# Hybrid encoder layer on eight cores: spatial gate in other PSUM banks, weight casts moved to a block's start, DMA transposes issued apart from their norm weights

## The chip, the cores and the metric

The kernel runs as one program on the 8 cores of one Trainium2 chip; every core has its own 10240 tokens, and the cores exchange nothing. A time is device microseconds (us) from start to end of the slowest core. The engines of a core are TensorE (PE, matmuls), VectorE (DVE), ScalarE (ACT), GpSimd (POOL) and SyncE (SP), and each works its own queue strictly in the program's order. A DMA is issued from a queue: here from SP, or from POOL where it changes the type.

## The reference, cut to what matters

```
h    = rmsnorm(x, norm_pre_mix)
proj = h @ W_in                       # [f | u | v | gate_a | gate_b], 512+512+512+1024+1024
u, v = gelu(u), gelu(v);  gate_a, gate_b = sigmoid(...), sigmoid(...)
y_a  = fourier_mix(f) @ w_fourier_out       # Re of a 2-D DFT
v    = layernorm(v)
y_b  = (u * (W_s v + b_s)) @ w_sgu_out      # spatial gate: W_s is 128x128 per group, in chunks of 128 positions
x    = x + rmsnorm((gate_a * y_a + gate_b * y_b) @ w_o, norm_post_mix)
h2   = rmsnorm(x, norm_pre_ffn)
up   = conv3(h2 @ w_up)                     # depthwise over positions
x    = x + rmsnorm((gelu(up[:4096]) * up[4096:]) @ w_down, norm_post_ffn)
```

D_MODEL is 1024, the mixer widths are 512, D_FF is 4096. Matmul operands are bf16, sums float32.

## The kernel before, in words

The program is written out in Python by `Prog.op`: each operation is appended to the queue of its engine, and waits are derived from the names that it reads and writes. So the order in the code is the order on each engine, and an operation that waits holds up everything behind it on its engine.

It has three stages. The Fourier stage (80 tiles of 128 tokens) ends in DRAM. The **mixer stage** is the loop `for p, i in enumerate(blocks)`: 20 blocks of 512 tokens, p = 0 to 19. The **channel stage** is 20 blocks of 32 column groups (`up`, `conv`), each followed by the down projection.

A mixer block p works so. SP loads `Yb` (the Fourier result) and the next block's four token tiles `xt`. PE forms four `u` chunks (`proj_chunk`, L838 to L844) and then four times a `v` tile (`v_tile`) and an output tile of block p-1 (`out_tile`). An output tile goes through `close_tile`: ACT squares it (L474), POOL takes the inverse root (L479, L481), DVE scales it (L924), POOL adds the residual `xr` (L929) and SP stores it to `x1s`. There are two `xr` buffers: the residual of tile 3 is loaded only after tile 1 is stored. ACT also squares the next block's tile (`pre_square`, L474 too). Behind tile 3's add POOL forms the next block's scales `rsd` (`pre_scale`: L479 and L481 on 128x4).

Then comes the gate phase, `for dc in range(8)`: chunk A (`winga`) and chunk B (`wingb`), each 8 matmuls into a bank that ACT empties by L843; in dc 0 and 1 also two spatial gates (`sgu_group`: 4 small matmuls, emptied by DVE L874, then DVE L881 with `uT`); and from dc = 2 the merge of dc - 2 (`merge_chunk`: 8 matmuls, DVE L891 and L895, POOL L898). In the text A0, B0, A1, B1 and so on are the gate chunks by dc. The banks: the projections and the spatial gates go round banks 1, 2, 3 (`wbank`); output tiles and merges use the pairs (4, 5) and (6, 7).

The next block is prepared inside the gate phase: `pre_cast(t)` (ACT L527) scales tile t to bf16 in `xs`, of which there are two, and waits for `rsd`; `pre_flip(t)` issues a DMA transpose from SP (L553) into `hT` and appends at once the DVE multiply with the norm weights (L555), which waits for that transfer. Casts stand at dc 2 to 5, flips at dc 3 to 6.

Blocks p = 1 to 3 also carry the second Fourier stage (`big_steps`), whose small matmuls use `wbank` too. From p = 4 each block converts a part of the channel stage's weights to bf16 in DRAM, by DMAs issued on POOL: `cast_wup` (L495, two DMAs) and `cast_wd` (L448). They stand behind `pre_scale`, at dc = 2 and at dc = 5.

Of the kernel before, what the change touches and what calls it, by code (L numbers as in the profile page):

```python
# [8 lines left out]
BF16 = mybir.dt.bfloat16  # L9
# [3 lines left out]
D = 1024  # L13
# [309 lines left out]
def build_program(cfg=None):  # L323
# [68 lines left out]

    NH = 2 * NBLK
    xt = [at(4 * k, D, F32, [("xt", k)]) for k in range(4)]
    xs = [at(16 + 2 * k, D, BF16, [("xs", k)]) for k in range(2)]
    hTb = [at(20 + 8 * k, 8 * 512, BF16, [("hT", k, t) for t in range(4)]).rearrange("p (k t) -> p k t", t=512)
           for k in range(2)]
    tt = [at(36 + 4 * k, D, F32, [("tt", k)]) for k in range(2)]
# [122 lines left out]
        s = pre_slot[par]  # L521
        inv_root(rsd[s][:, 0:4], ssq[s][:, 0:4], EPS, 4, [("ssq", s, t) for t in range(4)], ("rsd", s))

    def pre_cast(par, t):
        s = pre_slot[par]
        k = t % 2
        P.op("act", lambda e: e.activation(out=xs[k], in_=xt[t], func=AF.Copy, scale=rsd[s][:, t:t + 1]),  # L527
             reads=[("xt", t), ("rsd", s)], writes=[("xs", k)])

# [15 lines left out]
    def pre_turn(par, t, gvec, tbk=0):  # L545
        turn(t % 2, 128, hTb[par][:, :, t * 128:(t + 1) * 128], ("hT", par, t), gvec, tbk)

    def pre_flip(par, t, gvec):
        dst = hTb[par][:, :, t * 128:(t + 1) * 128]
        src = xs[t % 2]  # L550

        def flip(eng, sem):
            eng.dma_start_transpose(out=dst, in_=src).then_inc(sem, 16)  # L553
        P.op("sp", flip, reads=[("xs", t % 2)], writes=[("hT", par, t)], ndma=1)
        P.op("dve", lambda e: e.tensor_tensor(  # L555
            out=dst, in0=dst, in1=gvec.unsqueeze(2).broadcast_to([128, 8, 128]), op=ALU.mult),
            reads=[("hT", par, t), "cst0"], writes=[("hT", par, t)])

    def hres(par):
        return [("hT", par, t) for t in range(4)]  # L560
# [305 lines left out]
             reads=[("vg", k), ("mv", k), ("mvr", k)], writes=[("vhat", t)])  # L866

    def sgu_group(h):
        wb = wbank()
        for t in range(4):  # L870
            mm_group(bank(wb)[:, t * 128:(t + 1) * 128], [(vhat[:, t, h * 128:(h + 1) * 128], wstb[:, h, :])],
                     reads=[("vhat", t), "cstb"], writes=[("ps", wb)])
        k = ring("tmp", 4)
        P.op("dve", lambda e: e.scalar_tensor_tensor(  # L874
            out=tmp[k].rearrange("p (t q) -> p t q", q=128),
            in0=bank(wb).rearrange("p (t q) -> p t q", q=128),
            scalar=cst[:, C_LNG + h:C_LNG + h + 1],
            in1=bmat[:, h * 128:(h + 1) * 128].unsqueeze(1).broadcast_to([128, 4, 128]),
            op0=ALU.mult, op1=ALU.add),
            reads=[("ps", wb), "cst", "bmat"], writes=[("tmp", k)])  # L880
        P.op("dve", lambda e: e.tensor_tensor(out=uT[:, h, :], in0=tmp[k], in1=uT[:, h, :], op=ALU.mult),  # L881
             reads=[("tmp", k), ("uT", h)], writes=[("uT", h)])
# [108 lines left out]
    for p, i in enumerate(blocks):  # L991
# [10 lines left out]
        if p == 0:  # L1002
            next(big)
        else:
            pre_load(1 - par, nxt[0], nxt[1], nxt[2])
        for c in range(4):
            proj_chunk(par, winu, "winu", c * 128, uT[:, c, :], ("uT", c), AF.Gelu_apprx_tanh, 1.0)
            if p > 0:
                next(big, None)
# [15 lines left out]
            add()  # L1025
        if p > 0:
            pre_scale(1 - par)
        if p >= 4:
            cast_wup(1)
            cast_wd(1)  # L1030
        if p == NBLK - 1:
            ensure_loaded(NW - 1)
        for dc in range(8):
            h = dc // 2
            proj_chunk(par, winga, ("winga", h), dc * 128, ta[dc % NG], ("ta", dc % NG), AF.Tanh, 0.5)
            if dc < 2:
                sgu_group(2 * dc)
            if p > 0 or dc > 3:
                next(big, None)
            proj_chunk(par, wingb, ("wingb", h), dc * 128, tb[dc % NG], ("tb", dc % NG), AF.Tanh, 0.5)  # L1040
            if dc < 2:
                sgu_group(2 * dc + 1)
            if p == 0:
                if 1 <= dc < 5:
                    pre_square(1 - par, dc - 1)
                if dc == 4:
                    pre_scale(1 - par)
            late = 3 if p == 0 else 0
            if 3 + late <= dc < 7 + late:
                pre_flip(1 - par, dc - 3 - late, nxt[3])  # L1050
            if 2 + late <= dc < 6 + late:
                pre_cast(1 - par, dc - 2 - late)
            if dc >= 2:
                merge_chunk(dc - 2)
            if p > 0 or dc > 3:
                next(big, None)
            if p >= 4 and dc == 2:
                cast_wd(1)
            if p >= 4 and dc == 5:
                cast_wup(1)  # L1060
            if p == NBLK - 1 and dc == 7:
                halo_load(0)
        merge_chunk(6)
        next(big, None)
        if p == 0:
            pre_flip(1 - par, 2, nxt[3])
            pre_cast(1 - par, 3)
        merge_chunk(7)
        next(big, None)
        if p == 0:  # L1070
            pre_flip(1 - par, 3, nxt[3])


    cw4 = cst[:, C_CW:C_CW + 192].rearrange("p (h j t) -> p h j t", h=2, t=3)
# [74 lines left out]
    for i in range(NBLK):  # L1149
        more = i + 1 < NBLK  # L1150
        par = 1 - i % 2
        for j in range(32):
# [24 lines left out]
            if more:  # L1177
                if j in (8, 10, 12, 14):
                    pre_square(par, (j - 8) // 2)
                if j == 14:  # L1180
                    pre_scale(par)
                if j in (20, 22, 24, 26):
                    pre_flip(par, (j - 20) // 2, gpf)
                if j in (18, 20, 22, 24):
                    pre_cast(par, (j - 18) // 2)
        pending()
        pending = None
        r = ring_ctr.get("uppair", 0) % 3
# [115 lines left out]
```

## Time and profile before

| | us |
|---|---|
| median of 3 runs | 5149.03 |
| lowest and highest run | 5138.63, 6016.25 |
| the profiled execution's own time | 5129.78 |
| its span on the slowest core (core 6) | 5128.2 |
| spans of the 8 cores | 5085.4 to 5128.2 |
| mean granted TensorE clock of the cores | 0.992 to 0.994 |

The profile is one execution, seen on its slowest core. Outside the span lie 1.6 us. Its own time is 19 us under the median of the runs. In the rows an arrow points from what is waited for or read: `psum<-arena` writes PSUM from SBUF (the whole SBUF is one tensor, `arena`), and `[0.61 <-DVE arena L874]` is 0.61 us of idle time before the group, ended by the DVE instruction of line 874.

### The profile page before, as it was taken

The numbers are of one execution on the slowest core, as the hardware profiler recorded it, in microseconds if no ns is written. First come the engines' busy times: TensorE is split into PE (matmuls) and PEld (weight loads), VectorE is DVE, ScalarE is ACT, GpSimd is POOL, SyncE is SP. The second block draws the span as 40 slices with busy tenths as digits, with TensorE's granted clock in tenths as the row PEclk, the third lists the DMA queues.
The fourth block names the chain that finished last, engine by engine and source line by source line (L and its number), as shares of the span: only waits on it lengthen the run. The fifth ranks groups of instructions, "written<-read, shape, count | busy, mean of one in ns | idle before, by whom it ended". The sixth has DMA issues, their size and how long they took to land.

```text
span 5128.2 us, 81411 instructions; the slowest of 8 cores (5085.4 to 5128.2 us)
## 1 busy us (share of the span) xinstructions
PE 4970.4 (97%) x23976; PEld 2307.1 (45%) x24457; DVE 2786.6 (54%) x3917; ACT 2310.8 (45%) x3516; POOL 1984.9 (39%) x2480
## 2 busy tenths in 40 slices
PE   7889999999999999999999999999999999999999
PEld 4434444444444444444444444444444444444444
DVE  4635444444454475556645674557655674557554
ACT  5634433433333354445544554445544554445433
POOL 2323344443444433333433343334433343334333
PEclk9999999999999999999999999999999999999999
DMA  9794566555655574434534454445444454435432
GB/s 289 251 181 130 160 128 126 138 135 124 136 128 141 127 238 143 141 124 161 165 136 137 130 189 134 142 127 165 154 138 128 147 177 136 144 124 177 145 124 98
DMA packets 476173, 771.36 MB, mean 150 GB/s; under 512 B 285751, under 2 KB 310455, under 8 KB 474590
## 3 DMA queue, kind: packets, MB, share of 16 engines
q1 hardware_dynamic: 384526, 689.65, 43.3%
q0 software_dynamic: 91216, 76.46, 8.1%
q8 instruction: 210, 3.44, 0.3%
q14 instruction: 221, 1.81, 0.1%
HBM read 655.27 MB, written 130.02 MB: 153 GB/s over the span
## 4 chain that ended last, share of the span: by engine, by line
PE 89%; DMA 5%; issue 3%; POOL 1%; DVE 1%; ACT 1%; SPq 0%; POOLq 0%; DVEq 0%; ACTq 0%
PE psum L463 67%; PE psum L1194 21%; DMA arena<-arena 1%; DMA arena<-xf 1%; DMA arena<-xn 1%; ACT arena L474 0%; POOL arena L929 0%; PE psum L725 0%; DMA arena<-zbig 0%; DVE arena L874 0%; POOL arena L481 0%; DMA x1s<-arena 0%; DMA zbig<-arena 0%; POOL arena L714 0%; SPq L448 0%
## 5 line engine op out<-in xcount | busy, mean ns | idle before, releaser
L463 PE MATMUL psum<-arena 128*128 128x512 bf16 (+3 forms) x18278 | 3838.0, 369 | 108.2 <-DVE arena L874 15.3
L463 PEld LDWEIGHTS psum<-arena 128*128 128x128 bf16 (+1 forms) x18657 | 1767.3, 99 | 2152.4 <-issue 136.2
L1123 DVE SCALAR_TENSOR_TENSOR arena<-psum,arena 128x511 f32<-128x511 f32 x2560 | 1751.0, 743 | 348.7 <-ACT arena L1111 348.5
L1111 ACT ACTIVATE arena<-psum,arena 128x512 f32<-128x512 f32 x1280 | 993.2, 776 | 746.6 <-PE psum L463 746.6
L1133 POOL TENSOR_TENSOR arena<-arena 128x512 bf16<-128x512 bf16 x640 | 745.7, 1165 | 939.7 <-ACT arena L1131 922.1
L1194 PE MATMUL psum<-arena 128*128 128x512 bf16 x5018 | 1102.8, 379 | 5.4
L924 DVE SCALAR_TENSOR_TENSOR arena<-psum,arena 128x1024 f32<-128x1024 f32 x159 | 204.1, 1284 | 1154.6 <-POOL arena L481 1145.9
L1194 PEld LDWEIGHTS psum<-arena 128*128 128x128 bf16 x5120 | 500.9, 98 | 603.9
L474 ACT ACTIVATE arena<-psum 128x1024 bf16<-128x1024 f32 x160 | 163.8, 1024 | 1157.6 <-PE psum L1194 958.7
L843 ACT ACTIVATE arena<-psum 128x512 bf16<-128x512 f32 x400 | 238.5, 596 | 640.9 <-PE psum L463 609.7
L929 POOL TENSOR_TENSOR arena<-arena 128x1024 f32<-128x1024 f32 x159 | 377.0, 2371 | 189.9 <-DVE arena L924 126.6
L1131 ACT ACTIVATE arena<-arena 128x512 bf16<-128x512 f32 x640 | 397.0, 620 | 65.3 <-POOL arena L1128 64.2
L479 POOL TENSOR_SCALAR arena<-arena 128x1 f32<-128x1 f32 (+2 forms) x241 | 52.2, 216 | 946.8 <-ACT arena L474 940.5
L898 POOL TENSOR_TENSOR arena<-arena 128x512 bf16<-128x512 f32 x160 | 226.0, 1413 | 452.2 <-DVE arena L895 452.1
L555 DVE TENSOR_TENSOR arena<-arena 128x1024 bf16<-128x1024 bf16 x156 | 199.1, 1276 | 238.6 <-DMA arena<-arena 238.6
L1128 POOL TENSOR_TENSOR arena<-arena 128x4 f32<-128x4 f32 x640 | 197.0, 308 | 270.8 <-DVE arena L1123 265.2
L474 ACT ACTIVATE arena<-arena 128x1024 bf16<-128x1024 f32 (+1 forms) x241 | 253.3, 1051 | 38.1 <-DMA arena<-xf 26.9
L527 ACT ACTIVATE arena<-arena 128x1024 bf16<-128x1024 f32 x160 | 182.3, 1139 | 32.3 <-DMA arena<-arena 31.7
L891 DVE SCALAR_TENSOR_TENSOR arena<-arena,psum 128x512 f32<-128x512 bf16 x160 | 109.5, 684 | 127.8 <-PE psum L463 123.6
L481 POOL TENSOR_TENSOR arena<-arena 128x1 f32<-128x1 f32 (+2 forms) x241 | 159.3, 661 | 35.7
L854 DVE BATCH_NORM_STATS2 arena<-arena 128x6 f32<-128x512 f32 x80 | 54.9, 686 | 158.3 <-ACT arena L852 158.3
L895 DVE SCALAR_TENSOR_TENSOR arena<-arena,psum 128x512 f32<-128x512 bf16 x160 | 109.5, 684 | 12.7 <-PE psum L463 3.7
(45 smaller groups left out, 975.7 us busy)
## 6 DMA issues: line engine op xcount, KB each, us to landing
arena<-wups SPq DMA_DIRECT2D x640, 512.0 KB, 3.5
arena<-xn SPq DMA_DIRECT2D x160, 512.0 KB, 6.6
arena<-x1s SPq DMA_DIRECT2D x160, 512.0 KB, 5.5
arena<-xf SPq DMA_DIRECT2D x40, 1024.0 KB, 11.7
x1s<-arena SPq DMA_DIRECT2D x80, 512.0 KB, 3.2
y<-arena POOLq DMA_DIRECT2D x79, 512.0 KB, 4.0
wups<-w_up POOLq DMA_DIRECT2D x64, 256.0 KB, 5.2
arena<-yscr SPq DMA_DIRECT2D x20, 512.0 KB, 4.0
```

The costliest lines, as they stand in the source:

```text
L463: ins = e.matmul(out, lhsT=l, rhs=r, start=(i == 0), stop=(i == n - 1))
L474: P.op("act", lambda e: e.activation(out=sqjunk[:n, :], in_=src, func=AF.Square, accum_out=acc), reads=reads, writes=["sqjunk", accname])
L555: P.op("dve", lambda e: e.tensor_tensor(out=dst, in0=dst, in1=gvec.unsqueeze(2).broadcast_to([128, 8, 128]), op=ALU.mult), reads=[("hT", p ...
L843: P.op("act", lambda e: e.activation(out=dst, in_=bank(wb), func=func, scale=scale), reads=[("ps", wb)], writes=[dres])
L898: P.op("pool", lambda e: e.tensor_tensor(out=mT[:, dc, :], in0=tmp[k1], in1=tmp[k2], op=ALU.add), reads=[("tmp", k1), ("tmp", k2)], writes ...
L924: P.op("dve", lambda e: e.scalar_tensor_tensor(out=tt[k], in0=po, scalar=rsd2[s2][:, 0:1], in1=gpo, op0=ALU.mult, op1=ALU.mult), reads=pr ...
L929: P.op("pool", lambda e: e.tensor_tensor(out=xr[k2], in0=tt[k], in1=xr[k2], op=ALU.add), reads=[("tt", k), ("xr", k2)], writes=[("xr", k2)])
L1111: P.op("act", lambda e, half=half, b=b, c=c: e.activation(out=cv2[:, half, :], in_=bank(b), func=AF.Identity, bias=cst[:, C_CB + c:C_CB + ...
L1123: P.op("dve", lambda e, o_=o_, i_=i_, wt=wt: e.scalar_tensor_tensor(out=o_, in0=i_, scalar=wt, in1=o_, op0=ALU.mult, op1=ALU.add), reads=[ ...
L1131: P.op("act", lambda e: e.activation(out=gg, in_=cv2[:, 0, :], func=AF.Gelu_apprx_tanh), reads=[("cgv", k, 0)], writes=[("gg", k)])
L1133: P.op("pool", lambda e: e.tensor_tensor(out=actT[:, j, :], in0=gg, in1=cv2[:, 1, :], op=ALU.mult), reads=[("gg", k), ("cgv", k, 1)], writ ...
L1194: P.op("pe", lambda e, dh=dh: [e.matmul(bank(b0 + dh), lhsT=actT[:, j, t * 128:(t + 1) * 128], rhs=wd[j // 4][:, j % 4, dh * 512:(dh + 1) ...
```

## The change

It touches the mixer stage, and the channel stage's preparation of the next block.

- Spatial gate h goes to bank 4 + h (those of output tiles and merges) and no longer to the ring of banks 1 to 3.
- The four weight casts of a block (p from 4) are issued in one piece behind `pre_load`, ahead of the `u` chunks.
- `pre_flip` issues only the DMA transpose; the multiply is a function of its own, `pre_gain`.
- There are four `xs` tiles (two of them lie where the second Fourier stage had its buffer, so they are used from p = 4 on).
- For p = 4 to 18 cast and flip of tile t stand at dc = t (0 to 3) and the multiply at dc = t + 4. For p = 1 to 3 and 19: cast and flip at dc = t + 1, multiply at dc = t + 3, with two `xs`.
- In block p = 0 the transposes are made on PE again (`pre_turn`, 8 transposes of 128x128 and a DVE multiply out of bank 0).
- In the channel stage casts and flips stand one j earlier (17, 19, 21, 23), the multiplies where they were.

```
 def pre_cast(par, t, nx=2):            # xs[t % nx]
+def pre_gain(par, t, gvec):
     dst = hTb[par][:, :, t * 128:(t + 1) * 128]
-    src = xs[t % 2]
-    ...
-    P.op("sp", flip, reads=[("xs", t % 2)], writes=[("hT", par, t)], ndma=1)
     P.op("dve", lambda e: e.tensor_tensor(
         out=dst, in0=dst, in1=gvec.unsqueeze(2).broadcast_to([128, 8, 128]), op=ALU.mult), ...)
+def pre_flip(par, t, nx=2):
+    ...
+    P.op("sp", flip, reads=[("xs", t % nx)], writes=[("hT", par, t)], ndma=1)

 def sgu_group(h):
-    wb = wbank()
+    wb = 4 + h

@@ mixer block
+        if p >= 4:
+            cast_wd(1)
+            cast_wup(1)
+            cast_wd(1)
+            cast_wup(1)
         for c in range(4):
             proj_chunk(par, winu, ...)
@@
-        if p >= 4:
-            cast_wup(1)
-            cast_wd(1)
@@ for dc in range(8)
-            late = 3 if p == 0 else 0
-            if 3 + late <= dc < 7 + late:
-                pre_flip(1 - par, dc - 3 - late, nxt[3])
-            if 2 + late <= dc < 6 + late:
-                pre_cast(1 - par, dc - 2 - late)
+            if p == 0:
+                if 6 <= dc:
+                    pre_turn(1 - par, dc - 6, nxt[3])
+                if 5 <= dc:
+                    pre_cast(1 - par, dc - 5)
+            elif 4 <= p < NBLK - 1:
+                if dc < 4:
+                    pre_cast(1 - par, dc, 4)
+                    pre_flip(1 - par, dc, 4)
+                else:
+                    pre_gain(1 - par, dc - 4, nxt[3])
+            else:
+                ...
             if dc >= 2:
                 merge_chunk(dc - 2)
-            if p >= 4 and dc == 2:
-                cast_wd(1)
-            if p >= 4 and dc == 5:
-                cast_wup(1)
```

The order on ACT, for one block with p from 4 on, from the last output tile to the fourth cast. L474 are the squares, L843 the gate chunks in the order A0, B0, A1, B1 and so on, L527 the casts. Before:

```order
L474 ACTIVATE arena<-psum 128x1024
L474 ACTIVATE arena<-arena 128x1024
L843 ACTIVATE arena<-psum 128x512 x6
L527 ACTIVATE arena<-arena 128x1024
L843 ACTIVATE arena<-psum 128x512 x2
```

Now (L846 is what was L843):

```order
L474 ACTIVATE arena<-psum 128x1024
L474 ACTIVATE arena<-arena 128x1024
L846 ACTIVATE arena<-psum 128x512 x2
L527 ACTIVATE arena<-arena 128x1024
L846 ACTIVATE arena<-psum 128x512 x2
```

The first cast stood behind six gate chunks and now stands behind two.

The order on POOL, for the end of one block's preparation (L479 and L481 on 128x4 form `rsd`) and its eight merges (L898). Before:

```order
L929 TENSOR_TENSOR arena<-arena 128x1024 x2
L479 TENSOR_SCALAR arena<-arena 128x4
L481 TENSOR_TENSOR arena<-arena 128x4
L495 DMA wups<-w_up 1024x1x128 x2
L448 DMA wds<-w_down 16x8192
L898 TENSOR_TENSOR arena<-arena 128x512
L448 DMA wds<-w_down 16x8192
L898 TENSOR_TENSOR arena<-arena 128x512 x3
L495 DMA wups<-w_up 1024x1x128 x2
L898 TENSOR_TENSOR arena<-arena 128x512 x4
L857 TENSOR_SCALAR arena<-arena 128x1
```

Now (L932 was L929, L901 was L898, L860 was L857):

```order
L932 TENSOR_TENSOR arena<-arena 128x1024 x2
L479 TENSOR_SCALAR arena<-arena 128x4
L481 TENSOR_TENSOR arena<-arena 128x4
L901 TENSOR_TENSOR arena<-arena 128x512 x8
L448 DMA wds<-w_down 16x8192
L495 DMA wups<-w_up 1024x1x128 x2
L448 DMA wds<-w_down 16x8192
L495 DMA wups<-w_up 1024x1x128 x2
L860 TENSOR_SCALAR arena<-arena 128x1
```

All six cast DMAs of a block now stand between the last merge and the next block's first `v` tile (L860); `rsd` stands where it stood.

## Rows read from the trace of the kernel before

**Rows 1.** Busy time per stage; columns: window, length, busy of each engine, clock, DMA share, GB/s
```profile
560.00:1780.00 1220.00, 1184.55 (x5572) 545.29 (x5684) 568.93 (x746) 458.02 (x737) 543.16 (x594) 0.99 0.58 132
1780.00:5128.00 3348.00, 3311.70 (x15551) 1515.31 (x15862) 1936.44 (x2747) 1571.84 (x2309) 1269.52 (x1644) 1.00 0.45 147
```

**Rows 2.** What PE waited for, window 560 to 1780; us in total, times, longest
```profile
PE psum L463 <- DVE arena L874: 15.3, 22, 1.5
PE psum L463 <- DVE arena L891: 10.2, 6, 3.7
```

**Rows 3.** PE's work in order of time; start, us, matmuls, in brackets the idle before
```profile
333.61 9.42 PE L463 MATMUL psum<-arena 128*128 128x512 bf16 x43 [2.38 <-DVE arena L470]
349.19 1.44 PE L463 MATMUL psum<-arena 128*128 128x512 bf16 x3 [6.16 <-DVE arena L555]
...
661.11 48.91 PE L463 MATMUL psum<-arena 128*128 128x512 bf16 x219 [2.11 <-DVE arena L891]
...
1168.00 49.99 PE L463 MATMUL psum<-arena 128*128 128x512 bf16 x219 [3.65 <-DVE arena L891]
1218.60 4.06 PE L463 MATMUL psum<-arena 128*128 128x512 bf16 x24 [0.61 <-DVE arena L874]
...
1387.29 47.23 PE L463 MATMUL psum<-arena 128*128 128x512 bf16 x219 [1.79 <-DVE arena L891]
```

**Rows 4.** The window around one long wait of PE, same columns as rows 1
```profile
1162.00:1174.00 12.00, 8.30 (x25) 3.09 (x25) 7.62 (x10) 3.38 (x4) 4.96 (x3) 0.72 0.64 77
```

**Rows 5.** The chain that ended last, from two late flips; start, us, what
```profile
720.62 12.66 DMA arena<-arena
...
1150.71 15.22 DMA arena<-arena
```

**Rows 6.** All DMA transposes of the program: count, median us from issue to landing
```profile
arena<-arena SPq DMA_TRANSPOSE x156, 4.2
```

**Rows 7.** The gate phase's start in the block at 1214, all but PE in order of time
```profile
1213.63 0.33 SPq L448 DMA_DIRECT2D x1s<-arena  x1
1214.25 1.02 ACT L474 ACTIVATE arena<-psum 128x1024 bf16<-128x1024 f32 x1 [2.34 <-PE psum L463]
1216.36 0.33 SPq L448 DMA_DIRECT2D arena<-xn  x1
1216.51 1.28 DVE L924 SCALAR_TENSOR_TENSOR arena<-psum,arena 128x1024 f32<-128x1024 f32 x1 [1.31 <-POOL arena L481]
1217.87 0.60 ACT L843 ACTIVATE arena<-psum 128x512 bf16<-128x512 f32 x1 [0.78 <-PE psum L463]
1220.04 2.35 POOL L929 TENSOR_TENSOR arena<-arena 128x1024 f32<-128x1024 f32 x1 [1.31 <-DVE arena L874]
1223.13 1.02 POOL L481 TENSOR_TENSOR arena<-arena 128x4 f32<-128x4 f32 x1
1227.94 1.14 ACT L527 ACTIVATE arena<-arena 128x1024 bf16<-128x1024 f32 x1
```

**Rows 8.** The square of the last output tile and the end of rsd, two blocks
```profile
922.16 1.02 ACT L474 ACTIVATE arena<-psum 128x1024 bf16<-128x1024 f32 x1 [2.34 <-PE psum L463]
931.62 1.02 POOL L481 TENSOR_TENSOR arena<-arena 128x4 f32<-128x4 f32 x1
...
1136.08 1.02 ACT L474 ACTIVATE arena<-psum 128x1024 bf16<-128x1024 f32 x1 [2.34 <-PE psum L463]
1148.32 1.02 POOL L481 TENSOR_TENSOR arena<-arena 128x4 f32<-128x4 f32 x1
```

**Rows 9.** DMA in windows of one block: its start, the lull, the stores, the casts
```profile
1186.00:1198.00 12.00, 11.95 (x57) 5.43 (x56) 2.10 (x4) 2.99 (x5) 3.04 (x4) 1.00 0.81 307
1198.00:1208.00 10.00, 9.95 (x47) 4.57 (x47) 4.99 (x7) 5.50 (x10) 4.18 (x7) 1.00 0.00 0
1208.00:1216.00 8.00, 8.00 (x42) 3.75 (x40) 3.39 (x7) 4.41 (x8) 5.25 (x10) 1.00 0.53 197
1226.00:1237.00 11.00, 10.95 (x52) 4.96 (x51) 1.38 (x2) 4.78 (x7) 2.13 (x3) 1.00 1.13 134
```

More of the change, by code:

```diff
@@ L394, in build_program @@
     xt = [at(4 * k, D, F32, [("xt", k)]) for k in range(4)]
-    xs = [at(16 + 2 * k, D, BF16, [("xs", k)]) for k in range(2)]
+    xs = [at((16, 18, 60, 62)[k], D, BF16, [("xs", k)]) for k in range(4)]
     hTb = [at(20 + 8 * k, 8 * 512, BF16, [("hT", k, t) for t in range(4)]).rearrange("p (k t) -> p k t", t=512)
@@ L522, in pre_scale, with pre_cast @@
         inv_root(rsd[s][:, 0:4], ssq[s][:, 0:4], EPS, 4, [("ssq", s, t) for t in range(4)], ("rsd", s))
-    def pre_cast(par, t):
+    def pre_cast(par, t, nx=2):
         s = pre_slot[par]
-        k = t % 2
+        k = t % nx
         P.op("act", lambda e: e.activation(out=xs[k], in_=xt[t], func=AF.Copy, scale=rsd[s][:, t:t + 1]),
@@ L546, in pre_turn @@
         turn(t % 2, 128, hTb[par][:, :, t * 128:(t + 1) * 128], ("hT", par, t), gvec, tbk)
-    def pre_flip(par, t, gvec):
+    def pre_gain(par, t, gvec):
         dst = hTb[par][:, :, t * 128:(t + 1) * 128]
-        src = xs[t % 2]
-        def flip(eng, sem):
-            eng.dma_start_transpose(out=dst, in_=src).then_inc(sem, 16)
-        P.op("sp", flip, reads=[("xs", t % 2)], writes=[("hT", par, t)], ndma=1)
         P.op("dve", lambda e: e.tensor_tensor(
@@ L557, in pre_flip, with flip @@
             reads=[("hT", par, t), "cst0"], writes=[("hT", par, t)])
+    def pre_flip(par, t, nx=2):
+        dst = hTb[par][:, :, t * 128:(t + 1) * 128]
+        src = xs[t % nx]
+        def flip(eng, sem):
+            eng.dma_start_transpose(out=dst, in_=src).then_inc(sem, 16)
+        P.op("sp", flip, reads=[("xs", t % nx)], writes=[("hT", par, t)], ndma=1)
     def hres(par):
@@ L1047, in build_program @@
                     pre_scale(1 - par)
-            late = 3 if p == 0 else 0
-            if 3 + late <= dc < 7 + late:
-                pre_flip(1 - par, dc - 3 - late, nxt[3])
-            if 2 + late <= dc < 6 + late:
-                pre_cast(1 - par, dc - 2 - late)
+            if p == 0:
[10 more added lines that the diff above has]
+            else:
+                if 1 <= dc < 5:
+                    if dc >= 3:
+                        pre_gain(1 - par, dc - 3, nxt[3])
+                    pre_cast(1 - par, dc - 1)
+                    pre_flip(1 - par, dc - 1)
+                elif 5 <= dc < 7:
+                    pre_gain(1 - par, dc - 3, nxt[3])
             if dc >= 2:
@@ L1065, in build_program @@
         if p == 0:
-            pre_flip(1 - par, 2, nxt[3])
+            pre_turn(1 - par, 2, nxt[3])
             pre_cast(1 - par, 3)
@@ L1070, in build_program @@
         if p == 0:
-            pre_flip(1 - par, 3, nxt[3])
+            pre_turn(1 - par, 3, nxt[3])
     cw4 = cst[:, C_CW:C_CW + 192].rearrange("p (h j t) -> p h j t", h=2, t=3)
@@ L1182, in build_program @@
                 if j in (20, 22, 24, 26):
-                    pre_flip(par, (j - 20) // 2, gpf)
-                if j in (18, 20, 22, 24):
-                    pre_cast(par, (j - 18) // 2)
+                    pre_gain(par, (j - 20) // 2, gpf)
+                if j in (17, 19, 21, 23):
+                    pre_cast(par, (j - 17) // 2)
+                    pre_flip(par, (j - 17) // 2)
         pending()
```

## The prediction

> **What bounds the kernel now.** I read the stages by windows first, then the list of what PE waits for, then PE's work in order of time, and last ACT, POOL and the DMAs around the gate phase. The channel stage takes 3348 us of the span, and PE is busy for 3311.7 of them at a granted clock of 1.00 [rows 1]: what hides behind PE there can be moved freely, and nothing is to be won. The mixer window has 1220 us with 1184.6 busy, so 35.5 us in which PE waits [rows 1]. That is all that this change can take away there. Two entries make up most of it: 15.3 us in 22 waits on the spatial gate's emptying (DVE L874), and 10.2 us in 6 waits on the merge's emptying (DVE L891) [rows 2].
>
> The first comes from the ring of three banks. In the row at 1218.60 PE has idled 0.61 us for L874: the gate group holds the bank that the next gate chunk wants, and its emptying stands on DVE behind L924 of the last output tile [rows 3]. The list has 22 of them: one in each of the 16 blocks from p = 4 on, and a second one behind it in six.
>
> The second is a transfer. In two blocks the first flip took 12.66 and 15.22 us [rows 5], where the median of all is 4.2 [rows 6]. DVE stands at L555 for it with the merge's L891 behind, and PE runs out of banks: 2.11 and 3.65 us of waiting at 661.11 and 1168.00 [rows 3]. While the weight casts run, just before and under the flips, the DMA share is 1.13 [rows 9].
>
> **A wait has a price beyond its length.** Around the 3.65 us wait the granted clock is 0.72 over a window of 12 us [rows 4], so for part of it the chip granted 1.2 GHz where the rest ran at 2.4. The 219 matmuls behind it took 49.99 us and the 219 behind a 1.79 us wait took 47.23 [rows 3]: 2.8 us more. Behind the 2.11 us wait it is 48.91, which is 1.7 more. Behind 1.79 us, nothing was added.
>
> **The change part by part.**
>
> *Spatial gate in banks 4 to 7.* The ring waits go: 15.3 us [rows 2]. The new banks are those of output tiles 2 and 3, and L924 of tile 3 is over at 1217.79, 3.5 us after the gate phase's start [rows 7], ahead of gate 2's matmuls at 5.8 (three chunks and two groups, below), so no new wait. Saving 15.3.
>
> *Transposes apart from the multiplies, casts of weights elsewhere.* With the multiply four dc later (some 20 us) DVE no longer stands before a transfer. The 10.2 us [rows 2] go, and with them the clock's 1.7 and 2.8 us. Saving 14.7. The DVE work is the same and only later.
>
> *Block p = 0 on PE.* PE waited 2.38 and then 6.16 us for flips there [rows 3]. Four turns of 8 transposes are bounded by 0.2 us (nearly half of what eight matmuls of 128 columns take, so a floor) and 1.73 us (a whole chunk) apiece; I take 0.6, nearer the small matmuls, so 2.4 us. The last turn still needs the last cast and has a multiply behind it, so I leave a third of the 6.16 us standing at the start of block 1, 1.9 us. 8.5 less 4.3 is 4.2, and with 2.8 us of clock saved (one wait like the 3.65 one) it is 7.
>
> *The six cast DMAs of a block, now ahead of u.* POOL spends a few us on issuing them; it has nothing to do there, between the last merge and the first `v` tile. The transfers meet the loads of `Yb`, `xt` and `xr`, which fill 0.81 of the engines for 12 us, and then run into ten empty microseconds [rows 9]. In the window of the casts 1.13 of the engines were busy for 11 us, and this was more than half of a block's casts; I put a block's casts at 15 us of all engines. Loads (0.81 times 12, 9.7 us) and casts together are busy for 25 us, and the gate phase begins some 27 us after the block's start (1187 to 1214). So the casts' end comes close to the stores and loads of the residuals, which begin some 6 us before the gate phase (the window from 1208 [rows 9]). I take 0.5 us per block, 7 in all, as they overlap little; the bounds are 0 and what a late flip lost, 15.22 less 4.2, that is 11 us [rows 5, 6].
>
> On this the Trainium skill has a rule that weighs the other way than the row: "DMA: Bandwidth & Descriptors", section "Queues, rings and completion order", says that each DMA engine takes turns between the queues it has work for, packet by packet. By it a store could lose only about its own length to casts. The flips lost 8 to 11 us with the casts in flight, which is more than turns explain [rows 5, 6]. By the rule the sum has 7 us here or less, by the row it is the slower rival below.
>
> *The token casts at dc = 0.* This is the new wait. The first cast waits for `rsd`. In the block whose gate phase begins at 1214.25 (the square of the last output tile), `rsd` is ready at 1224.15, 9.9 us later, while ACT emptied chunk B0 at 1217.87 [rows 7]. Before, the cast came at 1227.94, behind six chunks, and so stood behind `rsd` anyway. Now it stands behind B0, and behind it on ACT stand A1 and B1. PE needs A1's bank for B2, since the ring has three banks and the gates no longer turn it. PE reaches B2 after five chunks of 1.73 us (8 of the 219 matmuls that take 47.23 [rows 3]) and four gate groups of 0.22 us (4 matmuls with a quarter of the columns): 9.5 us after the start. The bank is free at `rsd` plus the cast (1.14) plus the emptying (0.60): `rsd` plus 1.75. So PE waits (`rsd` - 7.75) us, in each of the 15 blocks p = 4 to 18.
>
> `rsd` cannot come sooner: it ends a chain of tile 1's add, its store at 1213.63, the load of tile 3's residual at 1216.36, the add at 1220.04 and the root [rows 7]. None of this is changed. By its distance the 15 blocks fall in three classes: six at 9.8 to 10.5 (the blocks at 1214 [rows 7] and 922 [rows 8]), three at 11.0 to 11.5, and six at 12.8 to 13.8 (1136 [rows 8]). The waits are 2.6, 3.5 and 5.5 us: 6 x 2.6 + 3 x 3.5 + 6 x 5.5 = 59 us. Nothing hides them, since PE is the engine that sets the end. To this comes the clock: 1.7 us for the six short ones and 2.8 for the nine others gives 35, of which I take 28, as a wait of 1.79 us cost nothing.
>
> *Blocks 1 to 3 and 19, and the channel stage.* Casts at dc = 1 instead of 2 stand behind four chunks, where the same rule gives B3 as the chunk that waits, at about 15.6 us, later than `rsd` plus 1.75 even in the slowest class. Zero, with a bound of 2 us each way in blocks 1 to 3. In the channel stage PE covers it all: zero.
>
> **The sum.** Saved: 15.3 + 14.7 + 7 = 37. Added: 59 + 28 + 7 = 94. Net 57 us slower. Against the profiled execution's 5129.8 this is 5187; that execution lies 19 us under the median of the runs, so on their scale 5206, and as the 7 of contention and the clock's part are my softest terms I say 5200, one per cent slower. This is under the 2% (103 us) that a measurement of this kernel can about tell from no change.
>
> **The rivals.**
>
> *A, the cast doesn't hold PE (5112).* The gains come alone: 5149 - 37. For it: ACT is busy for 458 us of the 1220 [rows 1] and has room to catch up. Against it: `rsd` is ready 9.9 us after the start at the soonest, ACT is at the cast after 4.2 [rows 7], and A1 stands behind it. Only an `rsd` 2 us sooner than in any block would do it. 12%.
>
> *B, the wait is there but always short (5155).* If the long class of `rsd` (12.8 and more) is itself made by transfers that the move of the casts smooths, all 15 blocks wait about 2.5 us: 38, with 5 us of clock: 43 - 37 is +6. For it: the short class is as common as the long one. Against it: the windows with store and load had no casts of this core beside them before either (they come at 1226 [rows 9]). 18%.
>
> *C, the casts reach the residual's chain (5280).* Place: store of tile 0 and load of tile 2, store of tile 1 and load of tile 3. If the casts still run 6 us before the gate phase and delay it as they delayed the flips, `rsd` comes 4 us later on average and every wait grows by that: 15 x 4 = 60, and the clock takes its 2.8 us in each block instead of 28 in all, 14 more: +57 + 74 = +131. It decides from where loads and casts together are busy for more than 21 us after the block's start; I reckoned 25 with them overlapping well. For it: rows 5. Against it: the casts are issued 20 us ahead of the chain. 15%.
>
> **How the numbers follow.** 55% for the forecast (its own range 5165 to 5240), 12% for A, 18% for B, 15% for C. The range 5122 to 5272 leaves out most of A and the upper half of C. Slower by over 2% is C and a little of the forecast's tail, 0.14; faster by over 2% would need more than PE waits in the whole stage, 0.01; within 2% has 0.85.
>
> **What would show it.** In the profile after: no wait of PE on the spatial gate's emptying (now L877) from p = 4 on; almost none on the merge's (now L894); a new first entry, PE waiting for ACT's gate emptying (L846), some 15 times with 2 to 6 us each, 59 us in all; ACT's first cast (L527) idle for 5 to 9 us on POOL L481; clocks under 1.00 in the mixer windows; the channel stage unchanged at 3312 us of busy PE. If PE waits on ACT for under 20 us in the mixer stage, the forecast's main step is wrong. If `rsd` comes 15 us or more after the gate phase's start, C is right.

## The result, and the profile after

The changed kernel is slower: 1.0177 times the kernel before, 95% interval 1.0101 to 1.0254. The interval leaves open whether it is more than 2%. Two of its runs took 5227.55 and 5242.54 us; the other two, of 5602 and 5859 us, fell into executions in which a die runs slower whatever the kernel, and such executions of this and every other kernel are left out of all ratios and times below. The profiled execution has a span of 5226.0 us on its slowest core, again core 6, against 5128.2: 97.8 us more. The forecast was 5200, or 1.0% slower; so direction and place came out, and the size did not: 98 us where the sum had 57.

The windows of the changed kernel, with the columns of [rows 1]; the mixer stage now ends near 1880:

```profile
560.00:1880.00 1320.00, 1213.04 (x5671) 549.14 (x5669) 579.72 (x742) 453.37 (x738) 575.89 (x594) 0.96 0.54 121
1880.00:5226.00 3346.00, 3325.70 (x15850) 1514.05 (x15848) 1939.60 (x2746) 1568.79 (x2306) 1264.94 (x1641) 1.00 0.45 147
```

All of the loss lies in the mixer stage. PE idles for 107 us of its window, where it was 35.5, and the granted clock has gone from 0.99 to 0.96. The channel stage is as long as it was, 3346 us to 3348, so what was moved there shows no cost and no gain.

What PE waited for in the mixer stage of the changed kernel, against [rows 2]:

```profile
PE psum L463 <- ACT arena L846: 104.2, 16, 7.5
PE psum L463 <- POOL arena L901: 2.5, 1, 2.5
```

Both old entries are gone, and one new one has come, almost seven times as large as the larger of them. PE's work in order of time shows it once a block, against [rows 3]:

```profile
642.11 72.01 PE L463 MATMUL psum<-arena 128*128 128x512 bf16 x336 [6.82 <-ACT arena L846]
...
1195.48 71.81 PE L463 MATMUL psum<-arena 128*128 128x512 bf16 x336 [7.14 <-ACT arena L846]
1274.13 71.73 PE L463 MATMUL psum<-arena 128*128 128x512 bf16 x336 [6.85 <-ACT arena L846]
```

The 336 matmuls of a block now run without any other break; in the fifteen blocks p = 4 to 18 the break before them is 5.6 to 7.5 us.

The gate phase of the block that begins at 1257.91 (the square of the last output tile), all engines but PE, against [rows 7]:

```profile
1252.12 0.33 SPq L448 DMA_DIRECT2D x1s<-arena  x1
1258.52 0.33 SPq L448 DMA_DIRECT2D arena<-xn  x1
1258.94 0.38 SPq L448 DMA_DIRECT2D x1s<-arena  x1
1261.53 0.60 ACT L846 ACTIVATE arena<-psum 128x512 bf16<-128x512 f32 x1 [0.78 <-PE psum L463]
1262.81 2.35 POOL L932 TENSOR_TENSOR arena<-arena 128x1024 f32<-128x1024 f32 x1 [2.74 <-DMA arena<-xn]
1264.07 0.33 SPq L448 DMA_DIRECT2D arena<-xn  x1
1267.94 2.88 POOL L932 TENSOR_TENSOR arena<-arena 128x1024 f32<-128x1024 f32 x1 [2.78 <-DVE arena L877]
1271.24 1.02 POOL L481 TENSOR_TENSOR arena<-arena 128x4 f32<-128x4 f32 x1
1272.36 1.15 ACT L527 ACTIVATE arena<-arena 128x1024 bf16<-128x1024 f32 x1 [10.23 <-POOL arena L481]
1273.41 1.06 ACT L846 ACTIVATE arena<-psum 128x512 bf16<-128x512 f32 x2
```

Read it from below. PE went on at 1274.13, when ACT had emptied chunk A1, the first of the two at 1273.41. ACT came to that only after the token cast, for which it had stood 10.23 us. The cast waited for `rsd`, ready at 1272.26, 14.35 us after the phase's start, where [rows 7] have 9.9 and the longest before was 13.8. And `rsd` was late because of the two stores. Tile 0's was issued at 1252.12, and the load that waits for its landing (tile 2's residual) went out only at 1258.52: 6.4 us. On SP tile 1's store stands behind that load, so it too went out late, and the pair of this store and tile 3's load has 1258.94 and 1264.07, 5.1 us; in [rows 7] it is 1213.63 and 1216.36, 2.7 us.

The block of [rows 7] is one of the quickest of the kernel before. The means of the blocks p = 4 to 18, both on core 6, times from the gate phase's start, read from all stores and loads of the residual chain:

| | before | changed |
|---|---|---|
| tile 0's store: issue, time to landing | -5.8, 3.4 | -5.7, 6.1 |
| tile 2's load: issue, time to landing | -2.2, 4.1 | 0.6, 4.3 |
| tile 1's store: issue, time to landing | -0.6, 3.9 | 1.0, 5.1 |
| tile 3's load: issue, time to landing | 3.4, 3.8 | 6.2, 3.7 |
| `rsd` ready | 11.6 | 14.2 |

Both stores are slower, and on this core the loads hardly are. The issuing of the casts is not the cause: POOL had done with it by 1236.97 and then stood idle for DVE:

```profile
1240.71 0.19 POOL L860 TENSOR_SCALAR arena<-arena 128x1 f32<-128x1 f32 x1 [3.74 <-DVE arena L858]
```

The DMA windows of this block, against [rows 9]: the two windows ahead of the gate phase, and then the clock around PE's wait.

```profile
1241.00:1251.00 10.00, 10.00 (x48) 4.58 (x47) 4.33 (x6) 5.49 (x10) 4.06 (x8) 1.00 1.24 250
1251.00:1259.00 8.00, 8.00 (x39) 3.63 (x38) 4.05 (x8) 3.83 (x7) 5.58 (x8) 1.00 0.89 138
...
1265.00:1280.00 15.00, 8.15 (x34) 3.31 (x33) 4.62 (x7) 5.28 (x7) 4.25 (x4) 0.77 0.47 140
```

The ten empty microseconds are filled (0.00 to 1.24) and the stores' window is at 0.89 instead of 0.53, with less moved: 138 GB/s for 197. The page has the weight casts (`wups`) landing in a median 19.7 us and all stores to `x1s` in 3.8:

```profile
x1s<-arena SPq DMA_DIRECT2D x80, 512.0 KB, 3.8
...
wups<-w_up POOLq DMA_DIRECT2D x64, 256.0 KB, 19.7
```

The same rows of the kernel before:

```profile
x1s<-arena SPq DMA_DIRECT2D x80, 512.0 KB, 3.2
...
wups<-w_up POOLq DMA_DIRECT2D x64, 256.0 KB, 5.2
```

### The profile page after: what moved, and what is told of

Same layout as the page of the kernel before. It is cut to its first block, busy times and chain, and to the rows that moved or that the text cites. A ratio compares the mean times of both kernels' runs of the same rounds, so it can differ in the third digit from the quotient of the medians.

```text
span 5226.0 us, 81993 instructions; the slowest of 8 cores (5195.2 to 5226.0 us)
## 1 busy us (share of the span) xinstructions
PE 5039.4 (96%) x24489; PEld 2322.5 (44%) x24489; DVE 2803.4 (54%) x3917; ACT 2304.7 (44%) x3516; POOL 2022.5 (39%) x2480
## 4 chain that ended last, share of the span: by engine, by line
PE 87%; DMA 7%; POOL 3%; issue 2%; ACT 1%; SPq 0%; DVE 0%; POOLq 0%; ACTq 0%; DVEq 0%
PE psum L463 65%; PE psum L1210 21%; DMA x1s<-arena 3%; DMA arena<-xn 2%; POOL arena L932 2%; DMA arena<-xf 1%; POOL arena L481 1%; DMA arena<-zbig 1%; PE psum L728 1%; SPq L448 0%; ACT arena L474 0%; DMA yscr<-arena 0%; POOL arena L479 0%; ACT arena L846 0%; POOL arena L717 0%
## 5 line engine op out<-in xcount | busy, mean ns | idle before, releaser
L463 PE MATMUL psum<-arena 128*128 128x512 bf16 (+3 forms) x18657 | 3904.1, 372 | 149.8 <-ACT arena L846 104.8
L474 ACT ACTIVATE arena<-psum 128x1024 bf16<-128x1024 f32 x160 | 163.8, 1024 | 1157.5 <-PE psum L1210 959.1
L846 ACT ACTIVATE arena<-psum 128x512 bf16<-128x512 f32 x400 | 236.3, 595 | 611.3 <-PE psum L463 611.2
L901 POOL TENSOR_TENSOR arena<-arena 128x512 bf16<-128x512 f32 x160 | 263.8, 1649 | 529.7 <-DVE arena L898 529.6
L932 POOL TENSOR_TENSOR arena<-arena 128x1024 f32<-128x1024 f32 x159 | 375.9, 2364 | 235.5 <-DVE arena L927 126.6
L479 POOL TENSOR_SCALAR arena<-arena 128x1 f32<-128x1 f32 (+2 forms) x241 | 49.8, 207 | 953.3 <-ACT arena L474 946.9
L474 ACT ACTIVATE arena<-arena 128x1024 bf16<-128x1024 f32 (+1 forms) x241 | 253.3, 1051 | 32.9 <-DMA arena<-xf 21.6
L527 ACT ACTIVATE arena<-arena 128x1024 bf16<-128x1024 f32 x160 | 182.2, 1139 | 163.6 <-POOL arena L481 159.6
L481 POOL TENSOR_TENSOR arena<-arena 128x1 f32<-128x1 f32 (+2 forms) x241 | 159.2, 661 | 36.0 <-POOL arena L479 1.4
L857 DVE BATCH_NORM_STATS2 arena<-arena 128x6 f32<-128x512 f32 x80 | 54.8, 685 | 156.0 <-ACT arena L855 156.0
L898 DVE SCALAR_TENSOR_TENSOR arena<-arena,psum 128x512 f32<-128x512 bf16 x160 | 110.0, 687 | 22.9 <-PE psum L463 9.6
## 6 DMA issues: line engine op xcount, KB each, us to landing
arena<-xf SPq DMA_DIRECT2D x40, 1024.0 KB, 11.3
wups<-w_up POOLq DMA_DIRECT2D x64, 256.0 KB, 19.7
```

What stands on the lines that cost most here:

```text
L463: ins = e.matmul(out, lhsT=l, rhs=r, start=(i == 0), stop=(i == n - 1))
L474: P.op("act", lambda e: e.activation(out=sqjunk[:n, :], in_=src, func=AF.Square, accum_out=acc), reads=reads, writes=["sqjunk", accname])
L481: P.op("pool", lambda e: e.tensor_tensor(out=out, in0=out, in1=neghalf[:p, 0:n], op=ALU.pow), reads=[name, "neghalf"], writes=[name])
L846: P.op("act", lambda e: e.activation(out=dst, in_=bank(wb), func=func, scale=scale), reads=[("ps", wb)], writes=[dres])
L901: P.op("pool", lambda e: e.tensor_tensor(out=mT[:, dc, :], in0=tmp[k1], in1=tmp[k2], op=ALU.add), reads=[("tmp", k1), ("tmp", k2)], writes ...
L932: P.op("pool", lambda e: e.tensor_tensor(out=xr[k2], in0=tt[k], in1=xr[k2], op=ALU.add), reads=[("tt", k), ("xr", k2)], writes=[("xr", k2)])
```

## The experiments

Theory 1 is the prediction's: the token cast at dc = 0 waits on ACT for `rsd` and holds chunk A1's bank, and the weight casts lengthen the wait by delaying `rsd`. Rival 2: the weight casts' traffic is the cost by itself. Further rivals stand with the runs. For e1, e6, e8 and e12 there is no ratio; they stand beside 5121 to 5166 us for the kernel before, and the verdict rests on the trace. No difference below, up or down, is clear of 2%; where an interval leaves out 1, its sign is shown. Where means of the eight cores are given, they are of one profiled execution of each kernel; the fifteen blocks are p = 4 to 18, from block 4's gate phase to block 19's.

### e1: token casts back at dc 2 to 5

```
-                if dc < 4:
-                    pre_cast(1 - par, dc, 4)
-                    pre_flip(1 - par, dc, 4)
-                else:
-                    pre_gain(1 - par, dc - 4, nxt[3])
+                if dc >= 4:
+                    pre_gain(1 - par, dc - 4, nxt[3])
+                if 2 <= dc < 6:
+                    pre_cast(1 - par, dc - 2, 4)
+                    pre_flip(1 - par, dc - 2, 4)
```

> The changed kernel, but for p = 4 to 18 the token casts and flips stand at dc 2 to 5 again (multiplies stay at dc 4 to 7). Theory 1 (the token cast waits for rsd on ACT and holds chunk A1's bank): the 104 us of PE waiting on ACT's gate emptying go, with some 30 us of half clock; what was won elsewhere stays, so a span of 5085 to 5110 and a time about 1% under the kernel before. The end of rsd stays at 13 to 15 us after the gate phase's start. Rival 2 (the weight casts ahead of u are the cost by themselves, through the loads that they meet): the time stays near the changed kernel's 5227.

Measured: 5095.09 us, span 5093.5. PE's work from 600 us on, slowest core:

```profile
599.70 534.05 PE L463 MATMUL psum<-arena 128*128 128x512 bf16 x2566
1134.63 210.16 PE L463 MATMUL psum<-arena 128*128 128x512 bf16 x1008 [0.88 <-ACT arena L846]
1344.98 280.02 PE L463 MATMUL psum<-arena 128*128 128x512 bf16 x1344 [0.19 <-ACT arena L846]
```

The first stretch is 2566 matmuls without a break. Moving four casts by two dc takes away 132 us, and the weight casts stand where the change put them: rival 2 is out. `rsd` was later here than I expected and than in the changed kernel (15.4 to 18.7 us after the start on this core, the 18.7 in the block before 1134.63), and only behind the three latest does the cast at dc 2 cost anything, 0.88 us at most.

### e2: weight casts back in their old places

```
-        if p >= 4:                       # ahead of u
-            cast_wd(1); cast_wup(1); cast_wd(1); cast_wup(1)
+        if p >= 4:                       # behind pre_scale
+            cast_wup(1); cast_wd(1)
...
+            if p >= 4 and dc == 2: cast_wd(1)
+            if p >= 4 and dc == 5: cast_wup(1)
```

> The changed kernel with the weight casts back where they stood before (behind pre_scale, at dc 2 and dc 5). Theory 1: rsd ends 9.8 to 13.8 us after the gate phase's start again (mean 11.7 instead of 14.2), PE still waits for ACT's gate emptying once in each of 15 blocks, 2 to 6 us each, 60 us in all; a span near 5175. Rival 2: PE's waits on ACT go, span 5090 to 5110.

Measured: 1.0083 (1.0051 to 1.0116), span 5177.4.

```profile
PE psum L463 <- ACT arena L846: 68.8, 16, 6.0
```

This is the prediction's main sum by itself: 69 us of waits in a kernel whose `rsd` is not delayed (a mean of 12.0 us on this core). The changed kernel has 35 us of waits more, which is what the weight casts' new place costs as long as the token casts stand early. Of the 49 us of span between the two slowest cores 32 lie in the fifteen blocks; in the mean of the eight cores it is 39 of 44.

### e3: gate banks alone

```
 def sgu_group(h):
-    wb = wbank()
+    wb = 4 + h
```

> The kernel before with the spatial gate in banks 4 to 7 and nothing else. Theory 1: PE's 15 us of waiting on the spatial gate's emptying go and no new wait comes, 15 us faster (0.3%). Rival 3 (the gate in the output tiles' banks makes a new wait on L924 or holds the first merges): PE waits for DVE L924 or for the gate's emptying at the first merges, no gain.

Measured: 1.0001 (0.9983 to 1.0020). Neither theory had it:

```profile
PE psum L463 <- DVE arena L891: 20.3, 9, 4.9
```

The waits on the gate's emptying are gone and there is none on L924, but those on the merge's emptying have doubled against [rows 2]. This is not the choice of core: in the mean of the eight cores the gate's go from 12.0 us to 0 and the merge's from 6.7 to 14.7, and the fifteen blocks take 1068.4 us for 1071.0. Most of the wait was passed on, not removed. The chain that ended last shows what stands before the longest of them, which ends at 945.46, a flip that lands late:

```profile
932.04 12.33 DMA arena<-arena
944.63 0.69 DVE arena L891
```

PE comes to the merges sooner, and DVE stands at the same late transfer.

### e4: weight casts alone

The kernel before with the move of the diff of e2, the other way round.

> The kernel before with the weight casts ahead of u and nothing else. Theory 1: rsd ends 2.5 us later on average (near 14.2 us after the gate phase's start), but the first token cast stands at dc 2 and PE does not wait for it; the flips no longer meet the weight casts, so the 10 us on the merge's emptying go: 5110 to 5125, the same or slightly faster. Rival 2: 60 to 100 us slower.

Measured: 0.9964 (0.9940 to 0.9988).

```profile
PE psum L463 <- DVE arena L874: 15.8, 25, 1.3
PE psum L463 <- ACT arena L843: 3.4, 1, 3.4
...
PE psum L463 <- DVE arena L891: 1.5, 1, 1.5
```

As theory 1 has it, but for the size of the delay: I expected `rsd` at 14.2 us, and it has a mean of 15.3 on this core (14.3 over the eight, where the kernel before has 11.3). The same move of the same DMAs is a small gain where the token cast stands at dc 2. Its waits on the merge's emptying fall to 1.5 us since the flips no longer meet the weight casts. In one block tile 0's store went out at 1324.91 and the load behind it only at 1335.96, 11.05 us later:

```profile
1324.91 0.33 SPq L448 DMA_DIRECT2D x1s<-arena  x1
1335.96 0.33 SPq L448 DMA_DIRECT2D arena<-xn  x1
```

`rsd` was 22 us after the start there, and PE waited 3.4 us for ACT, the only time.

### e5 and e6: rsd sooner

```
-        if add is not None:
-            add()
         if p > 0:
             pre_scale(1 - par)
+        if add is not None:
+            add()
```

e5 is the changed kernel with this edit alone; e6 also has the weight casts in their old places.

> The changed kernel with pre_scale ahead of the last output tile's add on POOL (the two statements change places), nothing else. Theory 1: rsd no longer waits for the residual of tile 3; it ends behind the add of tile 2, some 9.2 us after the gate phase's start (14.2 before), so PE waits under 2 us in each of 15 blocks, 15 to 30 us in all, with little half clock: a time of 5105 to 5135. Rival 4 (ACT's order alone costs the time, whatever rsd does): PE's 104 us of waits stay, 5227.

> As the run before, with the weight casts also back where they stood before. Theory 1: rsd ends some 6 us after the gate phase's start, before PE would run out of banks at 7.5, so PE does not wait for ACT at all in blocks 4 to 18: 5080 to 5100. Rival 4: 5175.

Measured: e5 0.9941 (0.9918 to 0.9965), e6 5092.24 and 5098.44 us. e5's waits, then e6's work of PE (in the execution of 5098.44):

```profile
PE psum L463 <- ACT arena L846: 8.4, 7, 2.9
```

```profile
599.76 1092.76 PE L463 MATMUL psum<-arena 128*128 128x512 bf16 x5252
1706.21 19.57 PE L463 MATMUL psum<-arena 128*128 128x512 bf16 x80 [13.69 <-ACT arena L846]
```

The token casts stand at dc 0 in both, and almost nothing is lost: it was not ACT's order alone but the order together with a late `rsd`. e5 did better than forecast (`rsd` at 9.2 us and 15 to 30 us of waits): `rsd` has a mean of 7.6 us, and the longest wait that is left is in the block where it is latest (10.5 us, 2.95 us of waiting). Two statements that change places turn 1.8% slower into 0.6% faster. In e6 `rsd` ends 6.3 us after the start in every one of the 15 blocks, and PE makes 5252 matmuls in one stretch. Its one wait is in block 19, where there are only two `xs` tiles: its four flips took 26 us on SP beside the weight casts, and the third token cast stood for them with PE behind it. The wait is there on all eight cores (10.5 to 14.4 us); e5, whose weight casts stand ahead of u, has at most 1.8 us.

### e7: block 0's turns alone

`pre_turn` for `pre_flip` in p = 0.

> The kernel before with block 0's transposes on PE and nothing else. Theory 1: the waits of 2.4 and about 6 us of block 0 shrink to about 2 us in all, 4 to 7 us faster (0.1%). Rival 5 (the turns' PE and DVE time eats it): no difference.

Measured: 1.0005 (0.9989 to 1.0022), which can't tell 5 us from none. In the trace:

```profile
329.36 3.61 PE L463 MATMUL psum<-arena 128*128 128x128 bf16 x12 [2.63 <-DMA arena<-zbig]
...
348.49 13.80 PE L463 MATMUL psum<-arena 128*128 128x512 bf16 x79 [2.07 <-DVE arena L541]
```

One wait of 2.07 us stands at the start of block 1 for the 6.16 of [rows 3], as forecast, and the one of 2.38 is gone, but one of 2.63 for a transfer of the second Fourier stage stands near it, and the turns themselves take PE 2.7 us (0.61 to 0.84 each). In the mean of the eight cores block 4 begins at 620.0 us for 621.4. That is 1.4 us, less than two kernels differ that are alike up to there (e4 has 624.4), so whether the turns gain anything stays open.

### e8 and e11: separate multiplies, with and without the gate banks

e8 joins the edits of e1 and e2; e11 has `wb = wbank()` again besides.

> The changed kernel with the token casts and flips at dc 2 to 5 and the weight casts where they stood before; gate banks, separate multiplies and block 0's turns stay. Theory 1: rsd ends near 12 us after the gate phase's start and the cast stands at 12, so PE waits neither for ACT nor for the gate nor for the merge in blocks 4 to 18, blocks of 70.0 us: 5085 to 5105. If this is so, the move of the weight casts brings nothing that the separate multiplies don't bring. Rival 6 (the flips need to be free of the weight casts): late flips still hold PE through the multiplies, 15 us or more of waits on DVE, 5115 or more.

> As e8, but the gates go round banks 1 to 3 again. Theory 1: the waits on the gate's emptying are back, 0.6 us in each block and about 15 us in all, and those on the merge's emptying stay away: 5100 to 5120. Rival 8 (what the gate banks save is given back elsewhere, as in the run with the banks alone): the same time as e8.

Measured: e8 5091.31 us, span 5089.8; e11 0.9924 (0.9885 to 0.9963), span 5110.0. First a wait of DVE in e8, then the longest of PE in e11:

```profile
DVE arena L550 <- DMA arena<-arena: 139.3, 17, 11.6
```

```profile
PE psum L463 <- DVE arena L877: 11.1, 18, 0.9
```

In e8 the flips are as late as before (up to 14.9 us to landing), and DVE still stands at the multiply for up to 11.6 us, but no wait of PE follows from it:

```profile
599.76 1099.66 PE L463 MATMUL psum<-arena 128*128 128x512 bf16 x5284
```

The 15 blocks last 69.7 to 70.2 us from gate phase to gate phase. So rival 6 is out, and e1 and e8 being alike (5095 and 5091), the move of the weight casts brings nothing beside the separate multiplies. In e11 the 0.6 us per block on the gate are back, and its blocks last 70.7 us and more. Between e11 and e8 (5101 and 5091 us in the shortest times, 1062.7 and 1049.5 us for the fifteen blocks in the mean of the eight cores) the gate banks are worth what e3 could not show, since there another wait took it up: rival 8 is not borne out.

### e12: early token casts with the gates in the ring

e2 with `wb = wbank()`.

> As e11 (gates in the ring, weight casts in their old places, separate multiplies, block 0's turns), but the token casts and flips stand at dc 0 to 3. Theory 1: now the fourth gate group wants chunk A1's bank, two chunks sooner than B2 did: PE reaches it some 8.2 us after the gate phase's start, and the bank is free 1.75 us after rsd, so PE waits about rsd minus 6.4, with rsd near 12 some 5 to 6 us in each of 15 blocks, 80 to 90 us in all (69 in e2), and more half clock: a time of 5190 to 5225. Rival 9 (the wait is set by the number of chunks ahead of the cast alone and not by the banks): as e2, 5177.

Measured: 5268.99 us on core 4, with a granted clock of 0.972. Cores 0 to 3 have spans of 5183 to 5210 us at 0.984 to 0.986, and core 3 is read; the forecast of 5190 to 5225 can be held only against these:

```profile
620.56 3.84 PE L463 MATMUL psum<-arena 128*128 128x512 bf16 x20 [0.60 <-DVE arena L877]
629.83 68.73 PE L463 MATMUL psum<-arena 128*128 128x128 bf16 x316 [5.44 <-ACT arena L846]
```

```profile
PE psum L463 <- ACT arena L846: 84.2, 16, 9.0
```

The 20 matmuls before the long wait are A1, a gate group and B1, and the first form behind it is 128x128: PE waits at the fourth gate group, 8.2 us after the start. With `rsd` at 11.8 us in that block the rule gives 5.4 us, and 5.44 were measured; the waits sum to 84.2. The bank that is wanted next sets when an ACT queue hurts. Rival 9 is out. In this one respect the gate banks protected the changed kernel.

### e10 and e9: what is left

e10 is e5 with the token casts at dc 2 to 5; e9 is e8 with `pre_scale` first.

> The changed kernel with pre_scale ahead of the last add on POOL and the token casts at dc 2 to 5: the version that leaves neither wait. Theory 1: no wait of PE on ACT in blocks 4 to 18, 5080 to 5095, the fastest of all by some us. Rival 7 (the weight casts at the block's start still cost through another queue): no faster than 5100.

> As e8 (token casts at dc 2 to 5, weight casts in their old places), with pre_scale ahead of the last add. Theory 1: rsd ends 6.3 us after the gate phase's start, far ahead of the cast at 11.7; blocks of 70.0 us as in e8, so no more than a few us from e8 and e10: 5085 to 5100. It tells whether anything is left to win from rsd once the cast stands late: by theory 1 nothing.

Measured: e10 0.9912 (0.9865 to 0.9959), e9 0.9948 (0.9926 to 0.9971); their shortest times are 5093.43 and 5098.6. Neither is below e8, and the forecast of e10 as the fastest of all failed. Its times, 5093 to 5105, lie on both sides of rival 7's 5100. A wait of PE in e10 on core 2, then one in e9 on core 3:

```profile
PE psum L463 <- DVE arena L884: 5.4, 5, 1.7
```

```profile
PE psum L463 <- ACT arena L846: 12.0, 1, 12.0
```

The first is for the product of gate and `uT`. In the mean of the eight cores it is 4.1 us in e10 and 2.4 in e1, and e8 and e9 have it on no core. The fifteen blocks take 1049.4 or 1049.5 us in e6, e8 and e9, with the weight casts in their old places, and 1052.8, 1055.1 and 1056.2 in e1, e10 and e5, with the weight casts ahead of u. So rival 7 is right in direction, at 3 to 7 us.

The second is block 19 again. With `rsd` at 6.3 us and the cast at 11.7 nothing is left to win in the blocks before it, as theory 1 said; they last 70.0 us in e9 as in e8. e1, e5, e6, e8, e9 and e10 lie between 5085 and 5099 in their shortest times, and the times do not rank them. All lie below every time of both kernels that is used here.

## Why the prediction was right or wrong

The difference of the two profiled executions, put together from the starts of the gate phases on core 6 (block 4's at 631.6 before and 625.9 after, block 19's at 1715.3 and 1807.8):

| | forecast | measured |
|---|---|---|
| up to block 4 (forecast: turns of block 0) | -7 | -5.7 |
| blocks 4 to 18, gate and merge waits, with their clock | -30 | -34 (15 blocks of 72.2 us to 70.0) |
| blocks 4 to 18, waits on ACT | +59, +7 with the delay | +101 (104.2 less 3.4 of block 19) |
| blocks 4 to 18, half clock behind them | +28 | +31 (what is left of 98.2) |
| from block 19 on | 0 | +5.3 |
| sum | +57 | +98 |

In the mean of the eight cores the three stretches are -7.4, +106.7 and +0.5 us: the middle one holds on every core, the other two differ from core to core by more than they measure here.

**The new wait: right in place, engine, number and rule.** It is at chunk B2 in all fifteen blocks, 9.4 us after the start, where the working had 9.5, and its length is the distance of `rsd` less 7.5, where the working had 7.75. Shown by e1 (cast moved, wait gone) and by e5 and e6 (`rsd` moved; 8.4 us and none left), and the rule forecast e12 for another order of banks.

**The step that failed is "The six cast DMAs of a block, now ahead of u"**, where I took 0.5 us per block. The distance of `rsd` grew on core 6 from a mean of 11.6 to 14.2 us: 2.6 us in each of fifteen blocks, and from 11.3 to 13.9 in the mean of the eight cores. e2 against the changed kernel gives 35 us of waits for it. e4 and e1 have the same move without the long waits, and a delay of 3.0 and 2.9 us in the mean of the eight cores (3.7 on e4's core 6), so the size is no constant of the move. Two things were wrong in it. I put the end of loads and casts 2 us ahead of the gate phase and then called the overlap small, though the chain of two stores and two loads begins 6 us ahead of it. And I priced the chain as if one transfer were slowed a little; tile 0's store takes 6.1 us for 3.4, and tile 1's, which stands behind the load that waits for it, starts 1.6 us later and takes 5.1 for 3.9. This was rival C's mechanism, at 2.6 us instead of the 4 that I gave it. So forecast and rival were one case and no alternatives: the sum with 2.6 us per block is 57 + 31 = 88. Of the 10 us still wanting on core 6, 5.3 are from block 19 on and 4 come from 7.5 in place of 7.75 in fifteen waits.

The Trainium skill's rule of taking turns packet by packet, in "DMA: Bandwidth & Descriptors", section "Queues, rings and completion order", would have let a store lose about its own length, if the packets of both queues are alike, which no run here shows. The mean of tile 0's store is within this, 2.7 us lost on 3.4, and the forecast should have had that value as its middle. Single stores lost more: the one at 1252.12 3.7 us on the 2.7 of [rows 7], and in e4 one took 10.9 us to its landing, so the trace does not bear the rule out as a bound.

**The clock: right in size, not in its rule.** 28 us were forecast. The 31 of the table are what is left over, but the rows bear them out: the 336 matmuls behind a wait take 71.4 to 73.1 us in the changed kernel, 2.1 more in the mean than the 70.0 of e8. The window around one of the waits is at 0.77, where [rows 4] have 0.72. The working, though, took the price to follow from the wait's length, with nothing up to 1.79 us. The waits are 6.7 us in the mean where 3.9 were forecast, and cost about the same each. And two rows of e5 have it the other way round, 2.95 us with nothing behind it and 2.13 us with 1.7:

```profile
633.98 70.12 PE L463 MATMUL psum<-arena 128*128 128x512 bf16 x336 [2.95 <-ACT arena L846]
706.23 71.81 PE L463 MATMUL psum<-arena 128*128 128x512 bf16 x336 [2.13 <-ACT arena L846]
```

So that the total came out is in part luck; what decides the price of one wait stays open.

**The savings: the sum right, the working not.** 37 was forecast and about 40 came on core 6 (in the mean of the eight cores e8 is 27 us under the kernel before), but not as independent terms. The 7 for block 0's turns are not borne out: e7 shows 1.4 of them, within the noise. Which part of the change brought the 5.7 up to block 4 is not shown. e3 shows the gate banks alone bring nothing, since PE's wait moves to the merges; e11 and e8 show them bring their part once the multiplies are apart. I had added two entries of a list of waits as if each could be taken out alone. And DVE does still stand before the transfers in e8; apart from the merges that costs PE nothing.

**Block 19: missed.** I gave it no wait. It has 3.43 us in the changed kernel, at B3 with `rsd` at 16.1 us, where `rsd` was later than any that I had looked at. My rule for B3 was right in form and 1 us off in place: PE reaches B3 14.6 us after the start and not 15.6 (the 9.5 of B2 and three more groups of eight matmuls at 1.73 make 14.7), so even the slowest class before would have waited about a microsecond.

**Rivals.** A fell: the cast does hold PE. B fell too: the moved weight casts do not smooth the chain of stores and loads, they slow it. C stands as said above.

## What to carry to other kernels

On an engine with an in-order queue an instruction may be moved ahead only as far as the time at which its inputs are there; what it then costs is not its own wait but what is queued behind it, and the price is read from who wants the next bank. When a value is wanted sooner, look first at what its own producer is queued behind: here two statements, scale before add, were worth 127 us between the profiled executions (spans of 5226.0 and 5098.7). And an empty stretch in the DMA rows is only free if the transfers put there also end in it.

## What the runs showed that I had not expected

- One edit is a gain of 0.4% or a loss of about 0.9% by the state of another: the weight casts ahead of u (e4; the changed kernel against e2).
- A 512 KB store beside the weight casts took a mean of 6.1 us instead of 3.4, and the casts themselves a median of 19.7 us instead of 5.2, while in the old place flips that met the same DMAs took 8 to 11 us more than the median. In both places the traffic delayed the transfers that something waited for.
- DVE waited 139.3 us for transfers in e8 with no wait of PE behind it, and 205 us before, with 10.2 us behind it; an engine's waiting time says little of its price.
